# The residual additions of the w_o stage, and the rest of GpSimd's share of the first feed-forward unit, on VectorE

## The reference

```python
mix = jnp.concatenate([rmsnorm(f_out, g_fout), rmsnorm(a_out, g_aout)], axis=-1) @ w_o
x = x + gate1 * mix
h2 = rmsnorm(x, g_ffn) * (1 + scale2) + shift2
ff = (jax.nn.silu(h2 @ w_gate) * (h2 @ w_up)) @ w_down
return x + gate2 * ff
```

## Time and profile before

| what | value |
|---|---|
| three runs | 1717.99 us median (1716.57 to 1720.53) |
| profiled execution | 1718.5 us |
| its span, first to last instruction | 1716.7 us |
| mean granted TensorE clock | 0.993 |
| busy PE, PEld | 1665.7 us (97%), 1325.3 us (77%) |
| busy DVE, ACT, POOL | 861.0 us (50%), 541.6 us (32%), 312.5 us (18%) |

### The profile page before, as it was taken

The page is one execution under the profiler, slowest core; times in us unless marked ns, Lnnn a source line. Parts: engine busy times, 40 slices in busy tenths (PEclk is TensorE's granted clock), DMA queues, the critical chain, the costliest instruction groups (busy, mean ns, idle before and its releaser), DMA issues.

```text
span 1716.7 us, 21256 instructions
## 1 busy us (share of the span) xinstructions
PE 1665.7 (97%) x8029; PEld 1325.3 (77%) x8029; DVE 861.0 (50%) x1255; ACT 541.6 (32%) x934; POOL 312.5 (18%) x263
## 2 busy tenths in 40 slices
PE   5899999999999999799999999999999999999999
PEld 2568888866667887688888888888888888788787
DVE  3714886068775457845354444535444533433533
ACT  3412332178873035512221221222122222222221
POOL 0301221078735556400000000000000000100101
PEclk8999999999999999999999999999999999999999
DMA  9660104064113022012112121211211554364462
GB/s 379 251 240 27 37 25 80 13 145 81 44 44 135 26 110 110 31 56 67 61 43 86 49 67 55 77 52 43 86 52 40 194 220 142 137 245 147 137 241 100
DMA packets 114891, 179.14 MB, mean 104 GB/s; under 512 B 22167, under 2 KB 62321, under 8 KB 111497
## 3 DMA queue, kind: packets, MB, share of 16 engines
q1 hardware_dynamic: 112969, 175.08, 30.4%
q10 hardware_dynamic: 1728, 3.15, 0.5%
q0 software_dynamic: 128, 0.02, 0.0%
HBM read 145.18 MB, written 33.05 MB: 104 GB/s over the span
## 4 chain that ended last, share of the span: by engine, by line
PE 74%; DVE 2%; issue 1%; DMA 1%; ACT 1%; POOL 0%; SPq 0%; DVEq 0%; POOLq 0%
PE banks L101 21%; PE banks L103 21%; PE banks L102 21%; PE banks L997 2%; PE banks L1027 2%; PE banks L1333 2%; PE banks L1006 2%; DMA f_raw<-ff_rows 1%; PE banks L1014 1%; PE banks L983 1%; POOL h_lo L1993 0%; PE banks L2052 0%; DVE t_raw L1924 0%; PE banks L1316 0%; DVE f_lo L1788 0%
## 5 line engine op out<-in xcount | busy, mean ns | idle before, releaser
L1788 DVE TENSOR_TENSOR f_lo<-f_raw,f_hi 128x2048 fp32r<-128x2048 f32 x66 | 115.3, 1788 | 214.9 <-ACT f_hi L1638 214.9
L101 PE MATMUL banks<-f_hi 128*128 128x512 f32 x528 | 205.7, 390 | 5.7 <-DVE ff_scratch L1960 5.7
L101 PE MATMUL banks<-h_hi,wff_hi 128*128 128x512 f32 x528 | 206.2, 391 | 0.1
L103 PE MATMUL banks<-h_hi,wff_lo 128*128 128x512 f32 x528 | 205.5, 389 | 0.0
L103 PE MATMUL banks<-f_hi,f_lo 128*128 128x512 f32 x528 | 205.4, 389 | 0.0
L102 PE MATMUL banks<-f_lo,f_hi 128*128 128x512 f32 x528 | 205.4, 389 | 0.0
L102 PE MATMUL banks<-h_lo,wff_hi 128*128 128x512 f32 x528 | 205.4, 389 | 0.0
L2003 POOL TENSOR_TENSOR x_back<-x_back,ff_scratch 128x512 f32<-128x512 f32 x18 | 24.6, 1393 | 973.2 <-DVE ff_scratch L1960 973.1
L101 PE MATMUL banks<-h_hi,win_hi 128*128 128x512 f32 x384 | 153.2, 399 | 5.9 <-POOL h_lo L361 4.9
L102 PE MATMUL banks<-h_lo,win_hi 128*128 128x512 f32 x384 | 149.8, 390 | 0.0
L103 PE MATMUL banks<-h_hi,win_lo 128*128 128x512 f32 x384 | 149.8, 390 | 0.0
(11 more groups left out here) (229 smaller groups left out, 3109.8 us busy)
## 6 DMA issues: line engine op xcount, KB each, us to landing
f_raw<-in_w_down SPq DMA_DIRECT2D x66, 512.0 KB, 4.7
f_raw<-ff_rows SPq DMA_DIRECT2D x33, 512.0 KB, 6.1
ada_rest<-in_w_ada SPq DMA_DIRECT2D x16, 1024.0 KB, 7.5
wff_raw<-in_w_gate SPq DMA_DIRECT2D x11, 1024.0 KB, 5.3
wff_raw<-in_w_up SPq DMA_DIRECT2D x11, 1024.0 KB, 5.3
ff_rows<-ff_act_late SPq DMA_DIRECT2D x44, 256.0 KB, 2.0
ada<-in_w_ada SPq DMA_DIRECT2D x8, 1024.0 KB, 16.3
win_raw<-in_w_in SPq DMA_DIRECT2D x16, 512.0 KB, 4.1
```

Of the source, the lines that this page charges most:

```text
L101: pe.matmul(out, lhs[0], rhs[0], start=start, stop=False)
L103: return pe.matmul(out, lhs[1], rhs[0], start=False, stop=stop)
L1788: dve.tensor_tensor(f2_lo[:, part, cols], f2_raw[:, part, cols], f2_hi[:, part, cols].bitcast(F32), ALU.subtract).then_inc(f2_ready, 1)
```

## The change

Five things are done, all in `second_half`. (1) The 48 additions to `x1` go from GpSimd to VectorE, each right behind the scaling of its bank. VectorE no longer waits for an earlier addition; it waits for the scaling itself to be written, and at the first bank of each chunk for the rows of x. (2) In the first unit the splits of the weight sums (`sum_lo`), the four `t4` and the eight splits of `h_raw` go from GpSimd to VectorE; one semaphore `t_lo` counts all token parts, in the order t2, first half of h, second half, t4, t3. ScalarE's copies stand in that order too. (3) The first unit's products come in the order p6, p5, p3, p4, p7. (4) Its four weight sums are cast and split in the order 1, 0, 3, 2. (5) In the down stage VectorE empties a chunk's banks before it splits the group after the next. GpSimd keeps the odd `lo` splits of chunks 0 and 1 and its additions in the down stage.

```diff
-    OPENING = ["a0", "p1", "a1", "p2", "p6", "p5", "p7", "p4", "p3"]
+    OPENING = ["a0", "p1", "a1", "p2", "p6", "p5", "p3", "p4", "p7"]
...
         for p in range(HK):
+            act.activation(h_hi[:, HK + p, TWO], h_raw[:, HK + p, TWO], ACT.Copy).then_inc(t_hi, 1)
+        for p in range(HK):
             act.wait_ge(t_added, 2 * HK + p + 1)
-            act.activation(t3_hi[:, p], t3_raw[:, p], ACT.Copy).then_inc(t_hi, 1)
-        for p in range(HK):
-            act.wait_ge(t4_added, p + 1)
             act.activation(t4_hi[:, p], t4_raw[:, p], ACT.Copy).then_inc(t_hi, 1)
         for p in range(HK):
-            act.activation(h_hi[:, HK + p, TWO], h_raw[:, HK + p, TWO], ACT.Copy).then_inc(t_hi, 1)
+            act.activation(t3_hi[:, p], t3_raw[:, p], ACT.Copy).then_inc(t_hi, 1)
...
             dve.wait_ge(o_summed, m + 1)
-            if m >= MR:
-                dve.wait_ge(x1_added, m - MR + 1)
             dve.scalar_tensor_tensor(mix_ring[:, m % MR], banks[:, m % 4], mix_rstd[:, 1, TT * half + t:TT * half + t + 1],
                                      gate1[:, REQ[t // 4], cols], ALU.mult, ALU.mult).then_inc(gated, 1)
+            if n == 0 and t % 4 == 0:
+                dve.wait_ge(x_in[t // 4], X1_IN)
+            dve.wait_ge(gated, m + 1)
+            dve.tensor_tensor(x1[:, t, cols], x1[:, t, cols], mix_ring[:, m % MR], ALU.add).then_inc(x1_added, 1)
...
-        for i, q in enumerate((1, 2, 0, 3)):
-            dve.wait_ge(s_added, 4)
+        dve.wait_ge(s_added, 4)
+        for q in (1, 0, 3, 2):
             dve.tensor_copy(s_hi[:, q], s_raw[:, q]).then_inc(s_hi_s, 1)
+        for i in range(3):
+            sum_lo(dve, 0, i)
...
             dve.tensor_tensor(t3_raw[:, p], last_rows, t1, ALU.subtract).then_inc(t_added, 1)
+            dve.wait_ge(t_added, 2 * p + 2)
+            dve.tensor_tensor(t4_raw[:, p], t3_raw[:, p], h_one[:, HK + p], ALU.subtract).then_inc(t4_added, 1)
+            if p == 0:
+                sum_lo(dve, 0, 3)
         for p in range(HK):
             dve.wait_ge(t_hi, p + 1)
-            dve.tensor_tensor(t2_lo[:, p], t3_raw[:, p], t2_hi[:, p].bitcast(F32), ALU.subtract).then_inc(t_lo_dve, 1)
+            dve.tensor_tensor(t2_lo[:, p], t3_raw[:, p], t2_hi[:, p].bitcast(F32), ALU.subtract).then_inc(t_lo, 1)
+        for half in range(2):
+            for p in range(HK):
+                dve.wait_ge(t_hi, HK * (half + 1) + p + 1)
+                low = slice(HK * half + p, HK * half + p + 1)
+                dve.tensor_tensor(h_lo[:, low, TWO], h_raw[:, low, TWO], h_hi[:, low, TWO].bitcast(F32), ALU.subtract
+                                  ).then_inc(t_lo, 1)
...
             c, jj = divmod(g, PAIRS)
             if jj < PAIRS - 1:
+                if g + 2 < GROUPS:
+                    down_lo(dve, g + 2)
                 continue
...
                     dve.tensor_tensor(x1_back[:, t, cols], x1_back[:, t, cols], scratch[:, m % 3], ALU.add).then_inc(d_added_dve, 1)
+            if g + 2 < GROUPS:
+                down_lo(dve, g + 2)
...
         for m in range(TT * OS):
-            add_mix(m)
             for c, first in enumerate(TURN):
                 if first <= m < first + 4:
                     split(KT * c + 2 * (m - first) + 1)
-        sums_lo(pool, 0)
...
                 elif name == "p7":
-                    pe.wait_ge(s_ready, 4 * u + 2)
+                    pe.wait_ge(s_ready, 4 * u + (4 if first else 2))
                     if first:
-                        pe.wait_ge(t_lo_dve, 2 * HK)
+                        pe.wait_ge(t_lo, 5 * HK)
```

More of the change, by code:

```diff
@@ L1433, in second_half @@
     x1_stored, X1_STORED = [*kept.u_stored, sem("x1_stored")], (24 * FT + 64, 24 * FT + 64, 64)
-    t_added, t4_added, t_hi, t_lo_dve, t_lo_pool = (sem(n) for n in ("t_added", "t4_added", "t_hi", "t_lo_dve", "t_lo_pool"))
+    t_added, t4_added, t_hi, t_lo = (sem(n) for n in ("t_added", "t4_added", "t_hi", "t_lo"))
     raw_in, w_hi_s, w_ready, summed, silu_ready = sem("wff_in"), kept.w_hi_s, kept.w_ready, kept.summed, kept.silu_ready
@@ L1776, in add_sums, with sum_lo @@
         plus(3, quarter(a_raw, 0, False), s_raw[:, 1], ALU.subtract)
-    def sums_lo(eng, u):
-        for i, q in enumerate((1, 2, 0, 3)):
-            eng.wait_ge(s_hi_s, 4 * u + i + 1)
-            eng.tensor_tensor(s_lo[:, q], s_raw[:, q], s_hi[:, q].bitcast(F32), ALU.subtract).then_inc(s_ready, 1)
+    def sum_lo(dve, u, i):
+        first = isinstance(u, int) and u == 0
+        q = ((1, 0, 3, 2) if first else (1, 2, 0, 3))[i]
+        dve.wait_ge(s_hi_s, 4 * u + i + 1)
+        dve.tensor_tensor(s_lo[:, q], s_raw[:, q], s_hi[:, q].bitcast(F32), ALU.subtract).then_inc(s_ready, 1)
     def down_lo(dve, g):
@@ L1815, in unit_dve @@
             add_sums(dve, u)
-            sums_lo(dve, u)
+            for i in range(4):
+                sum_lo(dve, u, i)
         if kind == UP:
@@ L1924, in run_dve @@
             dve.tensor_tensor(t3_raw[:, p], last_rows, t1, ALU.subtract).then_inc(t_added, 1)
+            dve.wait_ge(t_added, 2 * p + 2)
+            dve.tensor_tensor(t4_raw[:, p], t3_raw[:, p], h_one[:, HK + p], ALU.subtract).then_inc(t4_added, 1)
+            if p == 0:
+                sum_lo(dve, 0, 3)
         for p in range(HK):
             dve.wait_ge(t_hi, p + 1)
-            dve.tensor_tensor(t2_lo[:, p], t3_raw[:, p], t2_hi[:, p].bitcast(F32), ALU.subtract).then_inc(t_lo_dve, 1)
+            dve.tensor_tensor(t2_lo[:, p], t3_raw[:, p], t2_hi[:, p].bitcast(F32), ALU.subtract).then_inc(t_lo, 1)
[5 more added lines that the diff above has]
+                                  ).then_inc(t_lo, 1)
         for p in range(HK):
             dve.wait_ge(t4_added, p + 1)
-            dve.wait_ge(t_lo_dve, p + 1)
+            dve.wait_ge(t_lo, p + 1)
             dve.tensor_tensor(t3_raw[:, p], t3_raw[:, p], h_one[:, p], ALU.subtract).then_inc(t_added, 1)
         for p in range(HK):
-            dve.wait_ge(t_hi, 2 * HK + p + 1)
-            dve.tensor_tensor(t3_lo[:, p], t3_raw[:, p], t3_hi[:, p].bitcast(F32), ALU.subtract).then_inc(t_lo_dve, 1)
+            dve.wait_ge(t_hi, 3 * HK + p + 1)
+            dve.tensor_tensor(t4_lo[:, p], t4_raw[:, p], t4_hi[:, p].bitcast(F32), ALU.subtract).then_inc(t_lo, 1)
         for p in range(HK):
-            dve.wait_ge(t_hi, 3 * HK + p + 1)
-            dve.tensor_tensor(t4_lo[:, p], t4_raw[:, p], t4_hi[:, p].bitcast(F32), ALU.subtract).then_inc(t_lo_dve, 1)
+            dve.wait_ge(t_hi, 4 * HK + p + 1)
+            dve.tensor_tensor(t3_lo[:, p], t3_raw[:, p], t3_hi[:, p].bitcast(F32), ALU.subtract).then_inc(t_lo, 1)
         unit_dve(dve, 0, GATE, False)
@@ L1945, in run_dve @@
         for g in range(GROUPS):
-            if g + 2 < GROUPS:
-                down_lo(dve, g + 2)
             c, jj = divmod(g, PAIRS)
             if jj < PAIRS - 1:
+                if g + 2 < GROUPS:
+                    down_lo(dve, g + 2)
                 continue
@@ L2118, in unit @@
                         pe.wait_ge(gated, TT * OS)
-                        pe.wait_ge(t_lo_dve, HK)
+                        pe.wait_ge(t_lo, HK)
                     else:
@@ L2128, in unit @@
                 elif name == "p5":
-                    pe.wait_ge(s_ready, 4 * u + 3)
+                    pe.wait_ge(s_ready, 4 * u + (2 if first else 3))
                     if first:
-                        pe.wait_ge(t_lo_pool, HK)
+                        pe.wait_ge(t_lo, 2 * HK)
                     else:
@@ L2135, in unit @@
                     if first:
-                        pe.wait_ge(t_lo_dve, 3 * HK)
+                        pe.wait_ge(t_lo, 4 * HK)
                     else:
@@ L2139, in unit @@
                 else:
-                    pe.wait_ge(s_ready, 4 * u + 4)
+                    pe.wait_ge(s_ready, 4 * u + (3 if first else 4))
                     pe.wait_ge(p1_copied, u + 1)
                     if first:
-                        pe.wait_ge(t_lo_pool, 2 * HK)
+                        pe.wait_ge(t_lo, 3 * HK)
                 for k in range(KT if name in ("a0", "a1") else HK):
```

## The result

| what | before | after |
|---|---|---|
| runs | 1717.97 us median of 6 (1716.57 to 1720.53) | 1702.94 us median of 6 (1702.32 to 1705.00) |
| ratio of the runs | | 0.9914, 95% interval 0.9901 to 0.9927 |
| profiled execution, its span | 1718.5 us, 1716.7 | 1702.3 us, 1700.5 |
| granted clock, mean | 0.993 | 0.997 |

A forecast was written before the change was run, and what follows sets the result against it. TensorE, working nearly the whole span, was taken as the bound, so only its waits could be won back. 7.2 (first unit) + 6.1 (down stage) = 13.3; 1718.5 - 13.3 = 1705.2, said as 1705 us; range 1701.5 to 1709.5.

The forecast's parts named there:

- The first unit: First feed-forward unit: next unit starts at 711.5 against 718.70, a gain of 7.2 us with the normalisation losses included.
- 0.9 forecast: Normalisations of chunks 0 and 1: the reciprocal stands behind an addition, so TensorE loses 0.45 us twice.
- 1.4 each: First unit: TensorE waits 1.4 us ahead of p6 instead of 6.06, and a new 1.4 ahead of p4.
- The full clock in p6: p6 takes 2.72 us, not 4.46; rival: clock falls, costing 1.6 in p6, 3.2 at both waits, chance 0.11.
- The row with 1.00 in the earlier trace: Granted clock 1.00 about 2.89 us idle at 1467, cited as showing a wait this size does not lower the clock.
- the cover: Second unit's p1: last corner ends near 716.6, TensorE wants it at 716.9, so covered by 0.3 us.
- The reason for it: First unit: VectorE's steps are slow beside GpSimd; four `t_lo` subtractions take 5.69 us, against 2.48 with GpSimd still.
- The slower case: Rival: VectorE's dependent steps cost 1.67 us whatever GpSimd does, in w_o stage and first unit; 1723 us, chance 0.03.
- The eight `h_lo` splits left to GpSimd: w_o stage: each holds up a VectorE addition by at most 0.55 us; bank 3.5, still under TensorE's 3.6.
- The down stage: Two chunk ends: VectorE empties banks before splitting, removing two TensorE stops of 3.04 us, gain 6.1; giving nothing, chance 0.07.
- The sum: Whole kernel: 7.2 from the first unit and 6.1 from the down stage make 13.3 us.
- The step that missed: Whole kernel: 13.3 us taken off the profiled execution's 1718.5, everything else left as it was, giving 1705.2.

The follow-up runs named there:

- the twelve additions on GpSimd: The changed kernel with twelve unneeded 128x512 additions put on GpSimd in the first unit; 1713.21 us, ratio 0.9973.
- the memsets: The changed kernel with twelve unneeded 128x512 memsets on GpSimd in the first unit, writing SBUF and reading nothing; 1702.37 us, ratio 0.9909.

## Why the prediction was right

*The first unit*, forecast 7.2: from the normalisation of chunk 0 on the change has 0.50 and 0.46 lost (0.9 forecast); chunk 2's transposes come 0.34 late (0.35); p6 waits 1.51 and p4 1.10 (1.4 each); the next unit starts 9.96 us earlier, 708.74 against 718.70, of which 2.73 were there already when VectorE scaled the w_o stage's last bank ahead of chunk 0's normalisation. 9.96 - 2.73 = 7.2. The full clock in p6, on which 1.6 of it hung, came: in all eight profiles with the two short waits (0.87 to 1.51) p6 and p4 start at full speed. The reason given for it was weaker than it looked. The row with 1.00 in the earlier trace rows ends 0.04 ahead of TensorE's next matmul; the stretch behind the stop has 1.00 too (us, busy, granted clock, DMA share, GB/s):

```profile
1470.00:1474.00 4.00, 3.96 (x17) 1.00 0.80 296
```

But other executions took the half clock behind 2.34 and 2.66 us, so that one row did not show that such a wait is safe. How the 7.2 divide between GpSimd's work taken away and the new order of the products was not tried. The last corner ends at 713.22 + 0.68 = 713.90 and the second unit's p1 starts at 714.18 without a wait: the cover was 0.3 as worked out.

*The reason for it*, the two engines in each other's way, is shown by the twelve additions on GpSimd, and by the memsets, which change nothing. The slower case, a dependent step of 1.67 whatever GpSimd does, is refuted by the steps 0.72 apart. An addition starts 0.78 behind its scaling, not 0.71; a bank's work still ends well inside TensorE's 2.72. The eight `h_lo` splits left to GpSimd could hold up an addition by 0.55, the prediction says; they never met one. The twelve additions from 624 to 663 all take 0.69, and each of the six splits there ends 0.14 to 0.31 us ahead of the next addition, so the hold-up was not tried.

*The down stage*, forecast 6.1: 6.1 by the stretch of the kernel with this part alone, 6.4 by its runs.

*The sum* was short by 1.7 in the median and by 2.9 in the profiled pair. By the stretch the pair differs by 16.0; the attention takes 2.5 of that (from its first matmuls to chunk 0's normalisation 282.73 us before and 280.21 after, without the waits), and 13.5 are left for the parts that were added up, against 13.3. The step that missed is the one that left everything else as it was in the profiled execution: it held a slow start of the attention, 0.71, and that start was full in the changed kernel's three profiles. Whether the change itself makes the slow start rarer, or the executions fell that way, is open (five of five against three of nine), and so is how much of it lies in the runs' medians. In either case 13.3 agreed with the parts that it names, and the attention's 2.5 were not foreseen. Two places that take the half clock in some executions only, the attention's start and the stops at the chunk ends, belong in a range; 0.71 stood in the profile before.

## What to carry to other kernels

Moving work to an engine that is already late can make that engine earlier, if the other one reads SBUF beside its steps with two SBUF inputs: compare the same instruction's duration with the neighbour busy and still before counting instructions. A part that shortens no wait of TensorE's is worth nothing, however many instructions it moves: the 48 additions cost 0.4 us by the stretch in the changed kernel. Take the durations from more than one profile where TensorE's clock is below 1 in a place that the change doesn't touch.

## What was not expected of the hardware

Idleness of 2.34 and 4.36 us in one execution was followed by the half clock, idleness of 3.12 and 3.00 at the same places of the same kernel in another by the full one, and 2.36 to 3.17 in the three profiles of before by the full one too: a wait's length alone did not decide. The Trainium skill (TensorE: Matmul & The Clock Gate, Part 1) says that the clock gate has two states, and that the number of matmuls that one kernel runs at the lower clock at its start varies from run to run; the two profiles of one kernel differ in the same way behind waits far from the start. A memset of 128x512 on GpSimd took 0.53 us where a subtraction of the same size took 1.29, and left VectorE undisturbed.
